# Plain float32 products in place of float32r high/low pairs in a two-layer transformer with experts

## What is computed

```python
h = modulate(rms_norm(x, g_mix[l]), sh1, sc1)            # hc for the context in the same way
a_b, a_c, a_x, na_q, na_k, na_v, sw_q, sw_k, sw_v, ga, gb, gc = split_in(h @ w_in[l])
o_a = a_b * short_conv(a_c * a_x, conv_w[l])
o_b = neighbourhood_attention(...)                        # 8 heads of 64
o_c = window_attention(apply_rope(...), ...)              # 8 query heads, 2 key heads
x = x + gt1 * merge_branches((o_a, o_b, o_c), (ga, gb, gc), w_branch[l], w_out[l])
x = x + gt2 * expert_choice_ffn(modulate(rms_norm(x, g_ffn[l]), sh2, sc2),
                                w_router[l], w_exp_gate[l], w_exp_up[l], w_exp_down[l])
```

## Time and profile before

| | |
|---|---|
| median of 3 runs | 2043.54 us (2039.25 to 2044.04) |
| span of the profiled execution | 2033.6 us |
| TensorE busy | 1587.8 us (78%) |
| TensorE weight loads busy | 979.6 us (48%) |
| VectorE busy | 737.2 us (36%) |
| ScalarE busy | 487.0 us (24%) |
| GpSimd busy | 102.1 us (5%) |
| moved by DMA | 544.77 MB, 268 GB/s on the mean |

### The profile page before, as it was taken

One profiled execution on the slowest core, in us unless ns is written; L12 is line 12 of the kernel. 1 busy time (PEld: TensorE's weight loads), 2 busy tenths in 40 slices (PEclk: granted clock), 3 DMA queues, 4 the chain that ended last, 5 costly groups with the idle time before them and its releaser, 6 DMA issues.

```text
span 2033.6 us, 25423 instructions
## 1 busy us (share of the span) xinstructions
PE 1587.8 (78%) x10052; PEld 979.6 (48%) x10052; DVE 737.2 (36%) x1597; ACT 487.0 (24%) x1051; POOL 102.1 (5%) x149
## 2 busy tenths in 40 slices
PE   4999999889986978787787799889786565555654
PEld 1887777666664322222222598777673222222221
DVE  3356665655434112121211556766553010100102
ACT  3225555541242000000000435555250000000000
POOL 1002200000001000000000102200000000000000
PEclk8999999999997999999999899989988888888887
DMA  9332231126853999999999643345775999999996
GB/s 340 109 93 86 81 93 38 63 83 229 280 215 144 410 409 410 410 410 410 410 410 410 204 145 90 118 144 199 245 278 220 408 409 410 410 410 410 409 410 256
DMA packets 225060, 544.77 MB, mean 268 GB/s; under 512 B 8990, under 2 KB 99300, under 8 KB 224980
## 3 DMA queue, kind: packets, MB, share of 16 engines
q1 hardware_dynamic: 222580, 537.53, 69.9%
q0 software_dynamic: 2400, 6.16, 1.0%
HBM read 540.68 MB, written 2.98 MB: 267 GB/s over the span
## 4 chain that ended last, share of the span: by engine, by line
PE 37%; SPq 26%; DMA 13%; DVE 13%; ACT 7%; issue 5%; POOL 0%; DVEq 0%; POOLq 0%; ACTq 0%
SPq L878 25%; DMA ring<-in_w_exp_down 9%; PE bank L1658 7%; PE bank L1535 7%; PE bank L1537 7%; PE bank L1536 7%; DVE WL L1183 3%; PE bank L1686 3%; PE bank L1496 2%; DMA ring<-in_w_in 2%; ACT WH L1008 1%; PE bank L1626 1%; ACT PB L1081 1%; DMA ring<-in_w_ada 1%; DVE PB L1333 1%
## 5 line engine op out<-in xcount | busy, mean ns | idle before, releaser
L1658 PE MATMUL bank<-ring,XEB 128*32 128x256 f32 (+1 forms) x3072 | 392.1, 514 | 184.5 <-DMA ring<-in_w_exp_up 98.3
L1658 PEld LDWEIGHTS bank<-ring,XEB 128*32 128x32 f32 (+1 forms) x3072 | 143.8, 135 | 431.1 <-issue 174.3
L1535 PE MATMUL bank<-HH,WH 128*128 128x512 f32 (+1 forms) x864 | 308.0, 357 | 5.1 <-DVE WL L1183 4.5
L1536 PE MATMUL bank<-HL,WH 128*128 128x512 f32 (+1 forms) x864 | 303.5, 351 | 0.0
L1537 PE MATMUL bank<-HH,WL 128*128 128x512 f32 (+1 forms) x864 | 303.0, 351 | 0.0
L1658 PE MATMUL bank<-ring,HIDT 128*32 128x256 f32 (+1 forms) x1536 | 199.4, 522 | 79.0 <-DMA ring<-in_w_exp_down 67.6
L1183 DVE TENSOR_TENSOR WL<-ring,WH 128x1024 fp32r<-128x1024 f32 (+1 forms) x172 | 184.9, 1077 | 177.2 <-ACT WH L1008 176.5
L1008 ACT CAST WH<-ring 128x1024 fp32r<-128x1024 f32 (+1 forms) x172 | 158.0, 924 | 136.5 <-DMA ring<-in_w_in 59.6
L1535 PEld LDWEIGHTS bank<-HH,WH 128*128 128x128 f32 x864 | 167.1, 193 | 39.0 <-issue 14.5
L1448 DVE TENSOR_TENSOR YE<-bank,GT 32x512 f32<-32x512 f32 (+1 forms) x128 | 70.9, 554 | 301.1 <-PE bank L1658 299.8
L1537 PEld LDWEIGHTS bank<-HH,WL 128*128 128x128 f32 x864 | 166.7, 193 | 21.3
(11 more groups left out here) (190 smaller groups left out, 1782.2 us busy)
## 6 DMA issues: line engine op xcount, KB each, us to landing
ring<-in_w_exp_gate SPq DMA_DIRECT2D x64, 2048.0 KB, 23.5
ring<-in_w_exp_up SPq DMA_DIRECT2D x64, 2048.0 KB, 23.6
ring<-in_w_exp_down SPq DMA_DIRECT2D x64, 2048.0 KB, 23.7
ring<-in_w_ada SPq DMA_DIRECT2D x48, 1024.0 KB, 7.2
ring<-in_w_in SPq DMA_DIRECT2D x40, 1024.0 KB, 5.6
ring<-in_w_in SPq DMA_DIRECT2D x28, 512.0 KB, 4.9
ring<-in_w_branch SPq DMA_DIRECT2D x24, 512.0 KB, 6.2
ring<-in_w_out SPq DMA_DIRECT2D x8, 1024.0 KB, 7.9
```

The source lines that it names most:

```text
L1535: mm(t, wh, hi[:, k, 0:b.n], start=k == 0, stop=False)
L1536: mm(t, wh, lo[:, k, 0:b.n], start=False, stop=False)
L1658: last = mm(out_bank[tw * c:tw * c + tw, 0:nw], stationary[:, k, 0:tw], w[:, nw * c:nw * c + nw], start=k == 0, stop=k == KD - 1, tile_pos ...
```

## The change

The splits are gone. `H`, `O`, `MRG` and the ring's weights are used as float32 directly, and each step over k is one float32 product. A score is one product over the 64 rows of its head, in a row tile (`tile_position=(64 * hh, 0)`), from `QH` and `KH`/`KS`. The order of the four units of a set is changed from head by head to query tile by query tile. The gather multiplies `XN` itself. A chunk of the ring is released when the last block that reads it is done on TensorE (`used_tile`). The first loads of the experts' slots 4 and 5 wait for the end of attention in place of the end of the output blocks.

```diff
@@ finish_block, make_plan
         elif b.out in ("sk", "sq"):
             def rope():
                 b.rot_tile = P.tile(dve=True)
-                P.ropes += 1
-                b.rope = P.ropes
-                b.info.ready = ("qk_ready", P.ropes)
+                b.rope = True
+                b.qt_free, P.qt_free = P.qt_free, b.rot_tile.dve
+                b.info.ready += [("act_evicted", b.tile.act), ("dve_evicted", b.rot_tile.dve)]
                 P.add("finish", blk=b)
...
@@ attention, make_plan
-                for hh in range(2):
-                    for j in range(2):
+                for j in range(2):
+                    for hh in range(2):
                         units.append(Step(br=br, p=p, hh=hh, qt=2 * grp + j, u=P.units + len(units), info=info,
...
@@ end of make_plan
-    for l in range(DEPTH):
-        out, layer_blocks = [], [s.blk for s in P.steps[l] if s.kind == "k" and s.k == 0]
-        ahead = {a.b: c for a, c in zip(layer_blocks, layer_blocks[WAHEAD:])}
-        for s in P.steps[l]:
-            if s.kind == "k" and s.k == 0 and s.blk.b in ahead:
-                out.append(Step(kind="split", layer=l, blk=ahead[s.blk.b]))
-            if s.kind == "trmod" and s.which == 0 and s.k == 0:
-                out += [Step(kind="split", layer=l, blk=b) for b in layer_blocks[:WAHEAD]]
-            out.append(s)
-        P.steps[l] = out
+    for b in [s.blk for l in range(DEPTH) for s in P.steps[l] if s.kind == "k" and s.k == 0]:
+        b.chunk.used_tile = max(b.chunk.used_tile or 0, b.tile.ready)
     return P
...
@@ wait_released
-                elif o.used_tile:
+                else:
                     engine.wait_ge(blk_ready, o.used_tile)
-                else:
-                    engine.wait_ge(split_lo, o.split_end)
...
@@ block.sync, the first loads of the experts
-                                sp.wait_ge(blk_ready, s.c_tile if j < (4 if l == 0 else 5) else s.d_tile)
+                                if j < 4:
+                                    sp.wait_ge(blk_ready, s.c_tile)
+                                else:
+                                    sp.wait_ge(pv_ready, s.sets)
...
@@ block.scalar
-                    elif kind == "split":
-                        b = s.blk
-                        act.wait_ge(w_in[b.chunk.n], b.chunk.arrived)
-                        if b.b >= NWS:
-                            act.wait_ge(blk_ready, P.blocks[b.b - NWS].tile.ready)
-                        w = block_weights(b)
-                        nc.scalar.copy(WH[b.b % NWS][:, 0:b.kk, :], w).then_inc(split_hi, 1)
...
-                        if s.which == 0 and s.hts > 1:
-                            act.wait_ge(ht_ready, s.hts - 1)
                         sh, sc = (SH1, SC1) if s.which == 0 else (SH2, SC2)
-                        dst = FT[s.k % 2][:] if s.which == 0 else H2[:, s.k, :]
+                        dst = (H if s.which == 0 else H2)[:, s.k, :]
...
                         elif b.out == "nq":
-                            for hh in range(2):
-                                for half in range(2):
-                                    last = nc.scalar.activation(dup[b.p % 2][64 * half:64 * half + 64, 0, hh, 0:b.n],
-                                                                t[64 * hh:64 * hh + 64, 0:b.n], ACT.Copy, scale=HD ** -0.5)
-                            last.then_inc(act_evicted, 1)
...
+                            nc.scalar.activation(QH[b.p % 2][:, 0:b.n], t[:, 0:b.n], ACT.Copy, scale=HD ** -0.5).then_inc(act_evicted, 1)
...
-                        nc.scalar.copy(OH[l][ob][:, st.p, SEQ * st.grp:SEQ * st.grp + SEQ], PVB[:, 0:SEQ]).then_inc(o_hi, 1)
+                        nc.scalar.copy(O[l][ob][:, st.p, SEQ * st.grp:SEQ * st.grp + SEQ], PVB[:, 0:SEQ]).then_inc(o_ready, 1)
...
@@ block.vector
-                    elif kind == "split":
-                        b = s.blk
-                        dve.wait_ge(split_hi, b.b + 1)
-                        w = block_weights(b)
-                        nc.vector.tensor_tensor(WL[b.b % NWS][:, 0:b.kk, :], w, WH[b.b % NWS][:, 0:b.kk, :].bitcast(f32),
-                                                ALU.subtract).then_inc(split_lo, 1)
...
-                    elif kind == "trmod" and s.which == 0:
-                        dve.wait_ge(act_evicted, s.tile.act)
-                        link(nc.vector.tensor_copy(HH[:, s.k, :], FT[s.k % 2][:]))
-                        nc.vector.tensor_tensor(HL[:, s.k, :], FT[s.k % 2][:], HH[:, s.k, :].bitcast(f32), ALU.subtract).then_inc(ht_ready, 1)
...
@@ block.tensor
                         if k == 0:
                             open_tile(b.tile)
-                            pe.wait_ge(split_lo, b.b + 1)
+                            pe.wait_ge(w_in[b.chunk.n], b.chunk.arrived)
...
-                        mm(t, wh, hi[:, k, 0:b.n], start=k == 0, stop=False)
-                        mm(t, wh, lo[:, k, 0:b.n], start=False, stop=False)
-                        last = mm(t, wl, hi[:, k, 0:b.n], start=False, stop=k == b.kk - 1)
+                        moving = {"h": H, "m": MRG, "o0": O[l][0], "o1": O[l][1], "o2": O[l][0]}[b.src]
+                        last = mm(BLK[b.tile.bank][:, 0:b.n], block_weights(b)[:, k, :], moving[:, k, 0:b.n], start=k == 0, stop=k == b.kk - 1)
...
-                        for part in range(2):
-                            if x.br == "na":
-                                q, k = dup[x.p % 2][:, part, x.hh, q0:q0 + 128], stk[x.p % 2][:, x.hh, k0:TOK]
-                            else:
-                                q, k = stk[x.p % 2][:, x.hh, q0:q0 + 128], dup[0][:, part, x.p // 2, k0:TOK]
-                            last = mm(SB_[x.u % 2][:, 0:x.nk], q, k, start=part == 0, stop=part == 1)
+                        q0, k0, own = 128 * x.qt, TOK - x.nk, slice(64 * x.hh, 64 * x.hh + 64)
+                        keys = KH[x.p % 2] if x.br == "na" else KS[x.p // 2]
+                        last = mm(SB_[x.u % 2][:, 0:x.nk], QH[x.p % 2][own, q0:q0 + 128], keys[own, k0:TOK], start=True, stop=True,
+                                  tile_position=(64 * x.hh, 0))
...
                         for j in range(2):
-                            for part in (XNH, XNL):
-                                last = mm(t[:], part[:, 2 * s.s + j, 128 * s.k:128 * s.k + 128],
-                                          SELT[:, j, s.s, :, :].rearrange("p e t -> p (e t)"), start=j == 0 and part is XNH,
-                                          stop=j == 1 and part is XNL)
+                            last = mm(t[:], XN[:, 2 * s.s + j, 128 * s.k:128 * s.k + 128], SELT[:, j, s.s, :, :].rearrange("p e t -> p (e t)"),
+                                      start=j == 0, stop=j == 1)
```

More of the change, by code:

```diff
@@ L88, in __init__ @@
                  bias_before=None, blk=None, br=None, c_tile=None, chunk=None, code=None, col=None, d=None, d_tile=None,
-                 dve=None, end=None, expert=None, first=None, gate=None, grp=None, gt_free=None, half=None, hh=None, hts=None,
+                 dve=None, end=None, expert=None, first=None, gate=None, grp=None, gt_free=None, half=None, hh=None,
                  i=None, info=None, k=None, kind=None, kk=None, l=None, layer=None, lg=None, lt=None, mods=None, n=None, normalised=None,
                  nk=None, ns=None, ntt=None, o_ready=None, o_ready_need=None, ord=None, out=None, out_tile=None, p=None,
-                 parts=None, pt_before=None, qt=None, ready=None, recent=None, ref=None, rope=None, rot_tile=None, s=None,
-                 set=None, sets=None, slot=None, split_end=None, src=None, sum=None, tile=None, tiles=None, u=None, unit=None,
-                 units=None, used_tile=None, v=None, v_ready=None, which=None, width=None, x_updated=None, xnh=None):
+                 parts=None, pt_before=None, qt=None, qt_free=None, ready=None, recent=None, ref=None, rope=None, rot_tile=None, s=None,
+                 set=None, sets=None, slot=None, src=None, sum=None, tile=None, tiles=None, u=None, unit=None,
+                 units=None, used_tile=None, v=None, v_ready=None, which=None, width=None, x_updated=None):
         self.ac_tile = ac_tile
@@ L189, in __init__ @@
         self.bias_unit = [None] * 4
-        self.ropes = 0
+        self.qt_free = None
+        self.m_sums = {}
+        self.h_acts = [[] for _ in range(DEPTH)]
         self.obs = 0
@@ L240, in block @@
         self.blocks.append(b)
-        chunk.split_end = b.b + 1
         return b
@@ L331, in make_plan @@
         for k in range(KD):
-            P.add("trmod", which=0, k=k, ntt=4, tile=P.tile(act=True), mods=P.mods, hts=8 * l + k)
+            h_tile = P.tile(act=True)
+            P.add("trmod", which=0, k=k, ntt=4, tile=h_tile, mods=P.mods)
+            P.h_acts[l].append(h_tile.act)
         def col_chunk(name, l=l):
@@ L549, in make_plan @@
         for k in range(KD):
-            P.add("trmod", which=1, k=k, ntt=2 * ns, tile=P.tile(act=True), mods=P.mods, hts=None)
```

(23 more changed lines are left out.)

178 lines of the change are left out of this document (50 added, 128 removed).

## The result

| kernel | median of the runs | runs | profiled execution (span) |
|---|---|---|---|
| before | 2042.0 us (2039.3 to 2044.0) | 4 | 2033.6 us |
| changed | 2240.3 us (2237.0 to 2241.7) | 4 | 2239.9 us |

The ratio is 1.097 (95% interval 1.095 to 1.099), so the changed kernel is 9.7% slower, between 195 and 201 us. The forecast was 2250 us, the range 2205 to 2285.

The account below looks back on a forecast made before the run. DMA was taken to bound the expert stretches and TensorE the dense ones. The terms 152 + 32 + 14 + 19 - 44 - 8 + 42 gave +207 us on 2043.5 us, so 2250 us, range 2205 to 2285.

Parts of the forecast that it names:

- dense products: Dense steps over k: one float32 product (0.855 or 0.428 us) replaces three float32r products (0.680 or 0.360 us); +152 us.
- scores: Attention scores: two float32r products with 128 rows become one plain product with 64 rows; +32 us.
- row tile: Score in a 64-row tile between full products: 0.15 us extra for each of 96 scores; +14 us (0 to 29).
- gather: Gather ahead of the experts: four float32r products a tile become two plain ones, in both layers; +19 us.
- comes back: Dense stretches: of TensorE's 56.4 us idle, 44 return as VectorE and ScalarE queues lighten and TensorE's units lengthen; -44 us.
- starts: Both layer starts: H is written directly, without the wait for HL after two WH casts; -8 us.
- ring: Layer 0's stage C: six w_ada loads wait for places freed only at last product, 7 us each; +42 us.
- Expert stretches: Expert stages of both layers, DMA full: no product changed, so each keeps its length within 2 us.
- rival 2: Plain products cost more: 256-column halves wait on weight loads (31 us), row tile at upper end (15); about 2295 us; chance 0.14.
- rival 3: The two halves of a plain product overlap, so it costs one half; faster, about 1850 us; chance 0.02.
- rival 1: The ring does not stop TensorE, as loads come earlier or the wait hides; 2208 us; chance 0.14.
- rival 4: Attention: less idle time returns (30 us) or a new VectorE wait appears; 2265 us; chance beyond the spread 0.07.

Follow-up runs that it names:

- full rows: The changed kernel with score products reading all 128 rows of the query and key tiles, not one head's 64: 2204.3 us.
- the gather alone: The kernel before with only the gather's products made plain float32 from XN, and XNH, XNL and their subtractions gone: 2060.2 us.
- w_ada apart: The changed kernel with the w_ada chunks, all but the four of the start, in three 8 KB places of their own outside the ring: 2197.1 us.

## Why the prediction was right, and which of its terms were not

The direction, the size (+207 forecast, +198 by the medians) and the main mechanism hold. By its own steps:

| term | forecast | measured | by |
|---|---|---|---|
| dense products | +152 | +157 | steps of 0.859 and 0.432 us against 0.680 and 0.360 |
| scores | +32 | +32 | 0.86 us in the chain |
| row tile | +14 (0 to 29) | +36 | full rows, 2240.3 - 2204.3 |
| gather | +19 | +17.5 | the gather alone |
| comes back | -44 (-30 to -56) | -70 to -73 by the spans, -78 by the medians | what the sum leaves; idle time and clock |
| starts | -8 | -9 | starts of the stretches |
| ring | +42 (31 to 48) | +43 | w_ada apart, 2240.3 - 2197.1 |

**Expert stretches.** Unchanged in length, as said.

**Dense products.** Weight loads in order of time in layer 0 are 0.43 us apart (100.06, 100.49, 100.92 us), and 112 steps take 96.40 us in the chain, 0.861 each with what lies between the blocks:

```profile
45.45 96.40 PE bank L1411 x224
```

Taking 0.859 for 0.855 adds 672 x 0.004 = 3 us, and 0.432 for 0.428 adds 512 x 0.004 = 2 us. In layer 1 71 halves of 256 columns take 15.49 us; less the length of the last one (0.38 us) over 70, that is 0.216 a half. So rival 2's first half (256-column halves wait on the weight load) is wrong, and rival 3 (the halves overlap) is too.

**Row tile.** This term was mis-sized by 22 us, beyond its upper end, and rival 2's second half was nearer. The step that failed: I read the excess from the start of an ada step to the start of the product behind it. That interval holds neither the delay ahead of the tile's first product nor the slower first product behind the tile; both lie in the intervals beside it. Read over the whole turn, dense blocks included, the price is 0.39 us. The sign that the prediction gave for rival 2 has the same gap: the product after a score starts 1.06 us behind the score's start, 0.20 us late and under the 0.3 us of the sign, with the whole cost at 0.39. The Trainium skill, "TensorEngine Tiling (Array Packing)", section Key Properties, says that a change of the mode drains TensorE; by it a cost both on entry and on return was to be looked for, and the trace agrees, with 0.20 + 0.19 us.

**Comes back.** Mis-sized the other way, by 26 us or more. The sum of the two traces is 157 + 32 + 36 + 20 + 43 - 9 = +279 without this term (the gather by the traces), and the spans differ by 2239.9 - 2033.6 = 206.3, so about 73 us came back; with the 17.5 of the gather's own run it is 70, and with the medians' 198.3 it is 78. I kept 12 us of the 56.4 us of idle time; with w_ada apart only 3.4 + 1.7 = 5 are left, so 51 came back there. The other part I didn't count at all: the waits before had brought short stretches at the low clock (0.99 of 550 us and 0.97 of 350 us, which is 5.5 + 10.5 = 16 us of work lost). The same two stretches of the kernel with w_ada apart have 1.00. 51 + 16 = 67, so 3 to 6 us of what the spans leave have no place in this account. The reason given, both queues losing half of their work, wasn't needed in full: work of the weight splits' size on both queues changed nothing at the new pace. Layer 1 shows the miss in the prediction's own signs: its dense part was to be 35 to 45 us longer and was 390.2 - 356.7 = 33.5 us longer, while layer 0's (about 150) was 703.3 - 546.3 = 157.0 us longer, with five of the six stops in it.

**Starts.** The first dense product of layer 0 starts at 45.45 us, 4.7 us earlier. From the first expert product of layer 0 to the first dense product of layer 1 it is 1320.77 - 824.36 = 496.4 us against 500.5. Together 8.8 us.

**Ring.** There are six stops, as said, with the prediction's parts: 5.1 to 5.3 us from issue to landing, 1.7 us of slow ada step, and no wait for the w_in chunk behind. Four stand where it put them, at the second, fourth, sixth and eighth ada step. It put the other two at both ada steps after the fourth output block; they stand at the ada steps right behind the fourth and the eighth output block (712.25 and 754.08 us), and the one behind the sixth (731.74 us) runs without a stop. Rival 1 (no stops) is wrong, and rival 4 (less comes back) is as well.

**The base.** The sum was made against the profiled execution's 2033.6 us and set on top of the median, 10 us higher, as though these ten lay around the span. Only 1.8 us do: the changed kernel's profiled execution took 2241.7 us with a span of 2239.9, the gather alone's 2061.9 with 2060.1. The profiled execution of before was a quick one; its span and 1.8 us make 2035.4, where the fastest timed run took 2038.5. That is why the sum meets the difference of the spans (207 and 206.3) better than that of the medians (198), and why the forecast is 10 us too high. The profile of the gather alone shows where the time went, since its dense parts are those of the kernel before. From the first dense product to the last, with the columns of the earlier trace rows:

```profile
49.80:600.10 550.30, 524.30 (x2562) 400.04 (x2562) 290.51 (x664) 213.09 (x489) 33.63 (x48) 0.99 0.37 121
1169.80:1529.90 360.10, 329.09 (x2299) 283.69 (x2299) 223.81 (x501) 164.96 (x358) 24.33 (x36) 0.96 0.49 159
```

In the trace of before the same parts take 546.3 and 356.7 us, 7.4 us less. Idle time is nearly the same (57.0 us against 56.2); the clock isn't. To three digits it was granted 0.986 and 0.955 here and 0.991 and 0.968 there, so some 24 us of work were lost and not 16. With these figures 57 - 5 + 24 = 76 us could come back, against the 78 that the medians leave. Why one execution of the same code is granted less than another, no run shows.

So +207 came out right with two errors of opposite sign that nearly cancel: 22 us too little for the row tile, 26 us or more too little for what comes back. The direction and the main terms were reasoned; that the total came this close was luck.

## What to carry to other kernels

Where TensorE sets the pace, count its time per step first: a plain float32 product of 512 columns costs 0.86 us here and three float32r products 0.68, and no lighter queue beside it makes up for that. Read the price of a change of tile over a whole turn, both sides included, and give idle time its price in clock as well as in us. When a buffer's release moves from an early reader to the last one, walk the ring load by load: six loads of 1 MB whose place came free one step too late cost 43 us here, and a separate 24 KB a partition took that back.

## What the runs showed that I had not expected

- A 64-row tile between full products costs 0.39 us a time, nearly as much as a half product of 512 columns (0.43 us), in equal parts on the way in and on the way back.
- VectorE could carry 47% more work in layer 0's dense part up to the first stop (200 against 136 us) and 74% more in layer 1's (198 against 114) without a trace in the time, once TensorE's steps were 0.86 us long. At 0.68 us a step, taking work of that kind away (the weight splits) is worth 50 us.
- Taking 10 us of waits from one releaser gave nothing (0.9994): other releasers followed.
- GpSimd subtracts 128x1024 in 2.4 us, two times VectorE's time. The 19 us that this cost came with 29.3 us in which VectorE waited for masks behind the subtractions in GpSimd's queue.
- Executions of the same dense code differ by 7 us with the granted clock (0.986 and 0.955 against 0.991 and 0.968), at the same idle time.
